# Column units of a split-precision trunk: three 256-column products into one half bank, in place of one of 512 and one of 256

## The reference, cut to what matters

```python
proj = jnp.einsum("bsd,de->bse", h, w_in[i])
q, k, v, z, xbc, dt_raw, sc_b, sc_c, sc_h, gates = jnp.split(proj, offsets, axis=-1)
...
u = jnp.square(jax.nn.relu(jnp.einsum("bsd,df->bsf", hm, w_mlp_up[i])))
x = x + rms_norm(jnp.einsum("bsf,fd->bsd", u, w_mlp_down[i]), g_mlp_post[i])
```

## Time and profile before

| | |
|---|---|
| time, median of 3 | 1890.78 us (1890.68 to 1891.04) |
| the profiled execution | 1890.68 us, its span 1889.1 us |
| granted TensorE clock, mean | 0.998 |
| TensorE busy | 1873.3 us, 9514 matmuls, 9514 weight loads |
| VectorE, ScalarE busy | 1160.3 us, 944.9 us |
| memory traffic | 193 GB/s over the span |

### The profile page before, as it was taken

How to read it: one execution, slowest core, us unless ns; L and a number is a source line. 1 busy time by engine, 2 the same in 40 slices (tenths; PEclk the granted TensorE clock), 3 DMA queues, 4 the chain that set the end, 5 groups by cost and what they waited for, 6 DMA issues and landing times.

```text
span 1889.1 us, 27025 instructions
## 1 busy us (share of the span) xinstructions
PE 1873.3 (99%) x9514; PEld 1587.5 (84%) x9514; DVE 1160.3 (61%) x1304; ACT 944.9 (50%) x1140; POOL 50.9 (3%) x101
## 2 busy tenths in 40 slices
PE   9999999999999999999999999999999999999997
PEld 7888888888888888878888888888888888888886
DVE  7645555565656878875555666556545655565675
ACT  6544555545445677744444564344434443444464
POOL 1000000000000000000000000100000000000010
PEclk9999999999999999999999999999999999999999
DMA  7665555675565655555566566655566565556554
GB/s 253 221 224 178 177 174 172 211 217 194 191 196 181 228 179 193 170 189 189 190 211 192 172 213 213 192 194 186 192 193 190 188 191 197 186 180 192 176 190 143
DMA packets 100093, 364.62 MB, mean 193 GB/s; under 512 B 11560, under 2 KB 11704, under 8 KB 99608
## 3 DMA queue, kind: packets, MB, share of 16 engines
q1 hardware_dynamic: 96912, 351.32, 57.6%
q0 software_dynamic: 2960, 12.36, 1.9%
q10 hardware_dynamic: 160, 0.11, 0.0%
HBM read 361.60 MB, written 3.70 MB: 193 GB/s over the span
## 4 chain that ended last, share of the span: by engine, by line
PE 97%; ACT 1%; DMA 1%; DVE 1%; issue 0%; SPq 0%; DVEq 0%; ACTq 0%
PE ps L1467 29%; PE ps L1489 18%; PE ps L1491 17%; PE ps L1490 17%; PE ps L1471 14%; DMA w_raw<-w_stream 1%; PE ps L1683 0%; PE ps L1750 0%; DVE w_lo L738 0%; ACT w_hi L335 0%; PE ps L1705 0%; PE ps L1686 0%; PE ps L1671 0%; PE ps L1583 0%; PE ps L1594 0%
## 5 line engine op out<-in xcount | busy, mean ns | idle before, releaser
L738 DVE TENSOR_TENSOR w_lo<-w_raw,w_hi 128x1024 fp32r<-128x1024 f32 x661 | 806.9, 1227 | 599.4 <-ACT w_hi L335 596.6
L335 ACT ACTIVATE w_hi<-w_raw 128x1024 fp32r<-128x1024 f32 x661 | 692.8, 1057 | 686.4 <-PE ps L1491 480.3
L1467 PE MATMUL ps<-act,w_hi 128*128 128x512 f32 x2320 | 733.5, 397 | 1.7 <-DVE w_lo L738 1.0
L1471 PEld LDWEIGHTS ps<-act,w_lo 128*128 128x128 f32 x2320 | 435.8, 188 | 102.0
L1489 PE MATMUL ps<-w_hi,act 128*128 128x512 f32 x1328 | 518.3, 390 | 1.8 <-DVE w_lo L738 1.0
L1491 PE MATMUL ps<-w_hi,act 128*128 128x512 f32 x1328 | 516.8, 389 | 0.0
L1490 PE MATMUL ps<-w_lo,act 128*128 128x512 f32 x1328 | 516.7, 389 | 0.0
L1471 PE MATMUL ps<-act,w_lo 128*128 128x256 f32 x2320 | 457.3, 278 | 0.0
L1467 PEld LDWEIGHTS ps<-act,w_hi 128*128 128x128 f32 x2320 | 355.0, 189 | 4.3 <-issue 2.6
L1489 PEld LDWEIGHTS ps<-w_hi,act 128*128 128x128 f32 x1328 | 249.3, 188 | 54.1 <-DVE w_lo L738 1.8
L1491 PEld LDWEIGHTS ps<-w_hi,act 128*128 128x128 f32 x1328 | 249.3, 188 | 52.2
(11 more groups left out here) (234 smaller groups left out, 855.4 us busy)
## 6 DMA issues: line engine op xcount, KB each, us to landing
w_raw<-w_stream SPq DMA_DIRECT2D x662, 512.0 KB, 4.2
a_rows<-decay_rows POOLq DMA_DIRECT2D x8, 512.0 KB, 6.4
x_tok<-x_tok_in POOLq DMA_DIRECT2D x4, 512.0 KB, 5.4
x_T<-x_in SPq DMA_DIRECT2D x3, 512.0 KB, 10.0
out<-x_tok SPq DMA_DIRECT2D x3, 512.0 KB, 2.7
bias<-bias_rows POOLq DMA_DIRECT2D x8, 128.0 KB, 3.4
gain_mix<-gains_in POOLq DMA_DIRECT2D x1, 1024.0 KB, 8.4
gain_mlp<-gains_in POOLq DMA_DIRECT2D x1, 1024.0 KB, 6.4
```

The lines of the kernel that those rows point to most:

```text
L335: act.activation(whi[:, s, :], raw[:, s, :], ACT.Copy).then_inc(hi_ready, 1)
L738: dve.tensor_tensor(wlo[:, s, :], raw[:, s, :], whi[:, s, :], ALU.subtract)\
L1467: pe.matmul(bank[2 * g + t], whi[:, s, at_:at_ + P], a.rearrange("p a t -> p (a t)"), start=first and i == 0, stop=False)
L1471: mm = pe.matmul(bank[2 * g + t][:, T:2 * T], wlo[:, s, at_:at_ + P], a[:, 0, :], start=False, stop=last and i == len(kts) - 1)
```

## The change

In a column unit the 512-column matmul is cut in two of 256 columns, with the same stationary tile: high tokens, then low tokens. All three products of a set are added into the left half of the bank; the right half isn't used. A set of two tiles has six matmuls of 256 columns in place of two of 512 and two of 256; each has a weight load of its own. ScalarE's copies of the right halves are gone (72 of two tiles and the one of stage dt), and VectorE no longer adds two halves but copies one (`empty`), as soon as the block's last unit is done.

```diff
-                        pe.matmul(bank[2 * g + t], whi[:, s, at_:at_ + P], a.rearrange("p a t -> p (a t)"),
+                        pe.matmul(bank[2 * g + t][:, 0:T], whi[:, s, at_:at_ + P], a[:, 0, :],
                                   start=first and i == 0, stop=False)
+                        pe.matmul(bank[2 * g + t][:, 0:T], whi[:, s, at_:at_ + P], a[:, 1, :],
+                                  start=False, stop=False)
                     for t in range(tiles):
                         at_ = place(i, t)
-                        mm = pe.matmul(bank[2 * g + t][:, T:2 * T], wlo[:, s, at_:at_ + P], a[:, 0, :],
+                        mm = pe.matmul(bank[2 * g + t][:, 0:T], wlo[:, s, at_:at_ + P], a[:, 0, :],
                                        start=False, stop=last and i == len(kts) - 1)
...
-            def sum_to(dst, be, bc_, signal, uncopied=0):
-
-                g = bc_ % 2
-                dve.wait_ge(right_copied, be + (bc_ + 1 - uncopied))
-                dve.tensor_tensor(dst, pair[g][:, :, 0:T], right[:, g], ALU.add).then_inc(signal, 1)
+            def empty(dst, ue, uc, bc_):
+
+                dve.wait_ge(unit_done, ue + (uc + 1))
+                dve.tensor_copy(dst, pair[bc_ % 2][:, :, 0:T]).then_inc(block_done, 1)
...
-            def hidden(be, qe, b):
+            def hidden(ue, uc, qe, b):
 
                 g = (BLOCK0["mlp"] + b) % 2
-                dve.wait_ge(right_copied, qe + (UP_COPIES + b + 1))
-                dve.tensor_tensor(ev[:, b % 2], pair[g][:, :, 0:T], right[:, g], ALU.add).then_inc(up_summed, 1)
+                dve.wait_ge(unit_done, ue + (uc + 1))
+                dve.tensor_copy(ev[:, b % 2], pair[g][:, :, 0:T]).then_inc(up_summed, 1)
...
-                    copy_right(e, U + 4 * b + 3, be, B + b)
                     hidden(be, b)
```

More of the change, by code:

```diff
@@ L173, in build @@
     block_region = region(4)
-    right = place("right", [P, 2, 2, T], where=block_region)
     rowbuf = place("rowbuf", [P, 2, 512], where=block_region)
@@ L211, in build @@
         hi_ready, lo_ready, unit_done = sem("hi_ready"), sem("lo_ready"), sem("unit_done")
-        right_copied, block_done = sem("right_copied"), sem("block_done")
+        block_done = sem("block_done")
         x_loaded = [sem(f"x_loaded{i}") for i in range(4)]
@@ L340, in step @@
                 split_hi(e, c + LEAD)
-            def copy_right(ue, uc, be, bc_):
-                g = bc_ % 2
[L345 to L348, removed]
             def split_normed(j):
@@ L454, in _ @@
             step(0, U + 1)
[L455 to L458, removed]
             for name in ("ga", "gc"):
@@ L651, in quarter @@
                         if c >= 6:
-                            copy_right(0, U + c, 0, B + c - 6)
                             hidden(0, c - 6)
@@ L833, in _ @@
                 if c % 4 == 3:
-                    sum_to(qk[:, 2 * (c // 4):2 * (c // 4) + 2], 0, B + c // 4, block_done)
+                    empty(qk[:, 2 * (c // 4):2 * (c // 4) + 2], 0, U + c, B + c // 4)
             with dve.Fori(1, 4) as it:
@@ L838, in _ @@
                     if c % 4 == 3:
-                        sum_to(qk[:, ds(it * 4 + 2 * (c // 4), 2), :], it * 2, B + c // 4, block_done)
+                        empty(qk[:, ds(it * 4 + 2 * (c // 4), 2), :], it * 8, U + c, B + c // 4)
             dve.wait_ge(consts_loaded, 16)
@@ L875, in _ @@
                     if c % 4 == 3:
-                        sum_to(conv[:, ds(h * 4 + 2 * (c // 4), 2), :], h * 2, B + c // 4, block_done)
+                        empty(conv[:, ds(h * 4 + 2 * (c // 4), 2), :], h * 8, U + c, B + c // 4)
             U, B = UNIT0["dt"], BLOCK0["dt"]
@@ L881, in _ @@
             step(0, U + 1)
-            dve.wait_ge(right_copied, B + 1)
+            dve.wait_ge(unit_done, U + 2)
             dve.wait_ge(heads_loaded, 16)
-            dve.scalar_tensor_tensor(dt_raw[:, :], bank[2 * (B % 2)][0:SSM_HEADS, 0:T], head_consts[:, 0:1],
-                                     right[0:SSM_HEADS, B % 2, 0, :], ALU.add, ALU.add).then_inc(block_done, 1)
+            dve.tensor_scalar(dt_raw[:, :], bank[2 * (B % 2)][0:SSM_HEADS, 0:T], head_consts[:, 0:1], None, ALU.add)\
+               .then_inc(block_done, 1)
             def gate_branch(ue, uc, ge, gates, n, first):
@@ L1016, in _ @@
                 if c % 4 == 3:
-                    sum_to(ev[:, c // 4], 0, B + c // 4, block_done, BRANCHES)
+                    empty(ev[:, c // 4], 0, U + c, B + c // 4)
             U, B = UNIT0["ssd"], BLOCK0["ssd"]
@@ L1085, in group @@
                             dve.wait_ge(y_ssm_lo, g)
-                        sum_to(z[:, 0:2, :], g * 4, B, block_done, BRANCHES)
+                        empty(z[:, 0:2, :], g * 16, U + 3, B)
                     if c == 5:
@@ L1093, in group @@
                         dve.wait_ge(lo_ready, g * 16 + (U + c + 1 + LEAD))
-                        sum_to(z[:, 2:4, :], g * 4, B + 1, block_done, BRANCHES)
+                        empty(z[:, 2:4, :], g * 16, U + 7, B + 1)
                     if c == 9:
@@ L1105, in group @@
                     if c in (11, 15) and not last:
-                        sum_to(ev[:, c // 4 - 2], g * 4, B + c // 4, block_done, BRANCHES)
+                        empty(ev[:, c // 4 - 2], g * 16, U + c, B + c // 4)
                     if c == 14:
@@ L1273, in quarter @@
                         if c >= 6:
-                            hidden(0, 0, c - 6)
+                            hidden(0, U + c, 0, c - 6)
                 for b in range(2 * first, 8):
@@ L1283, in quarter @@
                                 dve.reciprocal(pre_rs[:, :], pre_rs[:, :]).then_inc(pre_inverse, 1)
-                    hidden(be, qe, b)
+                    hidden(e, U + 4 * b + 3, qe, b)
                 if first:
```

12 lines of the change are left out of this document (removed).

## The result

The changed kernel takes 1916.65 us, median of 4 runs (1916.46 to 1917.67), beside 1890.73 us for the kernel before on the same chip (4 runs, 1890.41 to 1891.04). The ratio is 1.0138, with a 95% interval of 1.0126 to 1.0150: 25.9 us slower. The forecast was 1883 us, faster. The time lies in the range of 1869 to 1919 us, but on the side to which 0.34 had been given.

The account below looks back on a forecast made before the run. TensorE was taken to bound the kernel (99% busy, 97% of the chain). From 1890.68 us, column sets gave -7.6 us and stage dt -0.1 us, hence 1883 us, range 1869 to 1919 us.

Parts of the forecast that it names:

- the price of the set: Column units: six 256-column matmuls at 0.115 us take 0.690 us against 0.6966 us, -7.6 us over 1152 sets.
- The bound below it: Column units: 256 columns take no less than 0.1133 us, so 0.680 us for a set, -19.1 us.
- Fixed cost for each matmul: Rival, column sets: 4.2 ns for each matmul makes a set 0.705 us, +9.7 us, 1900 us; chance 0.12.
- Loads set the pace: Rival, every column set: weight load plus handover hold matmuls to 0.12 us, +27.0 us, 1918 us; chance 0.20.
- Its sign: Profile after, column units: at 0.12 us or more per matmul, load rows stand end to end at the same pace.
- A stretch of one length runs like the row units: Rival, column units: 0.2267 us for each 512 columns, 0.680 us for a set, 1871 us; chance 0.25.
- The copies mattered: Rival, block ends: 72 copies of 0.6 us cost TensorE 43 us; held excluded beyond 1 or 2 us, no chance given.
- no new wait came up: TensorE: idle time ahead of column matmuls stays near 2 us; new waits for `lo_ready` or `block_done` would refute the prediction.
- the row part: Row units of an MLP quarter: should stay at 87.0 us.
- ScalarE's work: Block ends: 72 copies of 597 ns go, busy time falls by 43 us, nothing counted since ScalarE waits for TensorE.
- VectorE's copy: Block ends: the copy replacing the addition takes between 550 and 691 ns or a little over, covered by VectorE's waiting.
- The 3.8 us that tell a difference: Whole kernel: a measurement can tell about 0.2%, 3.8 us, from no change.

Follow-up runs that it names:

- stream128: Changed kernel with 128 columns streamed by each column matmul in place of 256, the other tokens left out: 2104.08 us, one run.
- cut_two_halves: Kernel before with only the 512-column matmul cut in two of 256; ScalarE's copies and VectorE's additions stay: 1916.98 us, ratio 1.0139.
- load32: Changed kernel with stationary tiles of 32 columns instead of 128, three quarters of the output features left out: 1891.35 us, one run.
- alternate: Kernel before with each set's matmuls ordered high, low, high, low instead of high, high, low, low: 1895.17 us, one run.
- row_cut: Kernel before with the row units' 512-column matmuls cut in two of 256, except the first of each accumulation; column units untouched: 1954.34 us, one run.
- all384: Kernel before with all four matmuls of a set at 384 columns: 1887.52 us, one run.
- grouped: Kernel before with each column unit's eight 512-column matmuls first, then its eight of 256 columns: 1892.45 us, ratio 1.0010.
- alt_entry: Kernel before with sets ordered high, low, high, low, but the old order in each block's first set: 1894.07 us, ratio 1.0018.
- alt_unit: Kernel before with sets ordered high, low, high, low, but the old order in each unit's first set: 1893.35 us, one run.

## Why the prediction was wrong

**The step that failed** is the price of the set: "I take 0.115 us, since it was read where pairs of 256 columns stand in the same units, with the same operands and slots; the other two need the surroundings to matter." The 256-column matmul costs 0.1200 us among its like, a set 0.7199 us instead of 0.690 us. That term was forecast at -7.6 us and measured at 1152 x 0.0233 = +26.9 us. The surroundings do matter: a distance between starts is not one instruction's price. In the kernel before the distance behind a short matmul was 112 to 120 ns, and behind a long one 230 to 236 ns instead of 227; what the short ones seem to save, the next long ones pay. Only a whole set or a stretch can be priced.

**The bound below it rested on the same slip.** "No row shows 256 columns faster than half of 0.2267 us" halves a number that has a fixed part. The prediction had both numbers for it: 0.2267 us for 512 columns, and the columns' own 512 / 2.4 GHz = 0.2133 us. The 13.4 ns between them, for one instruction, were never formed; instead 0.2267 us was taken as the price of 512 columns, and "the row units show none above 0.2267 us" was held against a fixed cost. With the fixed part 2320 more matmuls cost 2320 x 13.3 ns = 30.9 us, and 1152 sets of one length no longer pay the 3.3 ns that a mixed set had over its four fixed parts, 3.8 us: 27 us in sum. Read as a fixed part, six matmuls give 0.640 + 6 x 0.0133 = 0.720 us, and 1918 us. Even the set itself comes near: (0.6966 - 0.640) / 4 = 14.2 ns for each of four, so 0.725 us for six and 1923 us.

**The rivals.** *Fixed cost for each matmul* is the mechanism that the runs bear out; it was sized at 4.2 ns (1900 us), a third of what it is, for the reason above. The Trainium skill's rule (TensorE: Matmul & The Clock Gate, section Back-to-back issue gap), N / 2.4 + 2.5 ns, has this form too. The section gives it for a single isolated matmul and says that in a stream of loads and matmuls both set the spacing; the measured price beside the columns is 13.3 ns at 256, 384 and 512 columns here, not 2.5 ns. *Loads set the pace* named the right number, 0.120 us and 1918 us, but not by the mechanism, so that its fit would have been luck. Its sign, load rows at the pace of the matmuls, was there (0.12 us apart), but tells nothing, since every matmul has one load. Against it: with 128 columns streamed, loads went through at 0.1116 us each with no handover beside it, and longer matmuls, beside which a load has room, pay the same 13.3 ns. The same page of the Trainium skill (section LDWEIGHTS) has P / 1.2 ns for a load, an estimate of 107 ns; the 111.6 ns between loads in stream128 are near it. *A stretch of one length runs like the row units* was right as a sentence (both pay 13.3 ns for a matmul) and wrong in its price, since it scaled with the columns. *The copies mattered* is excluded: cut_two_halves keeps them and takes the same time.

**What held.** TensorE bounds the kernel, no new wait came up, the row part stayed at 87.0 us, ScalarE's work fell off without effect (36.8 us by its busy time, not 43: the lengths of its ACTIVATE rows do sum to 43.0 us less, but rows overlap their neighbours, and busy time counts an overlap once), and VectorE's copy took 692 ns, at the upper end named. The 3.8 us that tell a difference were far exceeded.

**What stays open** is what the 13.3 ns consist of. The runs with smaller tiles show that it is no fixed delay of the engine: for like instructions it can be 6.7, 11.1 or 13.3 ns within one run (load32), and 13.3 or 16.7 ns in another (alternate). With 128-column tiles and one length it was 13.3 ns wherever it was read, in both kinds of units; that is observed and not explained. Nor is it known why 256 columns pay only 6.7 ns in most stretches with a 64-column tile and never with a 128-column one. And in every run each matmul has a weight load of its own, so no run tells whether the 13.3 ns belong to the matmul or to the pair of load and matmul.

## What to carry to other kernels

Price a matmul as its columns at the clock plus a part for the instruction, and form that part from the kernel's own longest stretch of one kind: distance from start to start less N / 2.4. A cut that keeps the columns and adds instructions then costs about their number times that part (57.3 us of row_cut's 63.4, and here 30.9 us less the 3.8 that the mixed sets had lost). What it takes off engines that wait for TensorE anyhow gives nothing back, as the 43 us of copies show. Never take a single distance in mixed company as a price, and don't halve a number with a fixed part in it.

## What the runs showed of the hardware

**Several steady paces for the same instructions.** Unit by unit (16 or 24 matmuls), at a granted clock of 1.00; the last column is what is left for each matmul beside its columns:

| streamed, tile | one matmul, us | beside the columns, ns |
|---|---|---|
| 512, 128 (row units) | 0.2267 | 13.3 |
| 384, 128 (all384) | 0.1733 | 13.3 |
| 256, 128 (changed kernel, row_cut) | 0.1200 | 13.3 |
| 512 and 256 in pairs, 128 (before) | 0.1742 mean | 14.2 |
| the same, eight and eight (grouped) | 0.1746 mean | 14.6 |
| the same, one by one (alternate) | 0.1733 or 0.1767 mean | 13.3 or 16.7 |
| 512, 64 | 0.2300 | 16.7 |
| 384, 64 | 0.1733 or 0.1767 | 13.3 or 16.7 |
| 256, 64 | 0.1133 or 0.1200 | 6.7 or 13.3 |
| 256, 32 | 0.1133, 0.1178 or 0.1200 | 6.7, 11.1 or 13.3 |

A stretch mostly keeps its pace as long as nothing in the order changes. Which pace it gets depends on what was ahead of it in alt_entry and alt_unit, where a reordered set switched it; for the other runs this is not shown. A shorter load does not by itself make a matmul cheaper: at 384 and 512 columns the 64-column tile was no quicker than the 128-column one, and a 32-column tile had the 0.1200 us of the 128-column one in one stretch. But at 256 columns only the smaller tiles had anything quicker.

**Half the clock at 100% busy.** With 128 columns streamed, the granted clock was 0.50, so 1.2 GHz, from 65 to 575 us, while TensorE was shown busy without a gap. What it had done before, from 54 to 64 us, was column units of 128-column matmuls at the pace of their loads, with 1.4 us of idle time in them (the kernel before idles 1.0 us in the same place, and kept its clock). The clock rose soon after row units of 512 columns had begun, at 574 us. At the low clock the starts are 0.21 us apart:

```profile
299.74 0.41 PE L1440 MATMUL ps<-act,w_hi 128*128 128x128 f32 x1
299.95 0.41 PE L1442 MATMUL ps<-act,w_hi 128*128 128x128 f32 x1
```

Half the columns, and the kernel took 2104 us. In the MLP, where row units of 512 columns come ahead of them, the same matmuls ran for 85.7 us without a break at the full clock. What tells the two cases apart is not shown.

**A loss that shows at the joint.** row_cut lost some 6 us more than its matmuls account for. The ends of two quarters have waits of 2.4 and 2.7 us that the kernel before does not have, and behind the second the granted clock was 0.51 for 6 us, which cost 2.9 us more. A slower pace in one part can cost a second time where two parts meet, and an idle stretch there a third time by the clock.
